# Hybrid decoder step with 32 experts: the residual summed in PSUM with the experts' rows, final norm read from PSUM, 64-column one-hot rows

## The reference

```python
t = rmsnorm(x2, ln_ffn)                      # 320 x 1024
grp = argmax(t @ rg_w + rg_b)                # one of 4 groups of 8 experts
top_v, top_i = top_k(le[grp], 2)             # two experts of that group
for e in range(32):                          # D_EXPERT = 512
    hid = silu(t @ w_gate[e]) * (t @ w_up[e])
    acc = acc + combine[:, e:e+1] * (hid @ w_down[e])
y = rmsnorm(x2 + acc, ln_final)
```

## Time and profile before

| | |
|---|---|
| median of three runs | 837.72 us |
| profiled execution | 836.28 us, span 834.6 us |
| PE busy | 780.1 us, 93% |
| DVE, ACT, POOL busy | 33%, 19%, 17% |
| granted TensorE clock, mean | 0.972 |
| read from HBM | 246.6 MB, 306 GB/s over the span |

### The profile page before, as it was taken

One profiled execution on the slowest core, in us unless ns is written; L12 is line 12 of the kernel. 1 busy time (PEld: TensorE's weight loads), 2 busy tenths in 40 slices (PEclk: granted clock), 3 DMA queues, 4 the chain that ended last, 5 costly groups with the idle time before them and its releaser, 6 DMA issues.

```text
span 834.6 us, 8869 instructions
## 1 busy us (share of the span) xinstructions
PE 780.1 (93%) x3528; PEld 376.1 (45%) x3528; DVE 274.1 (33%) x618; ACT 160.4 (19%) x321; POOL 139.5 (17%) x168
## 2 busy tenths in 40 slices
PE   4999999989899999579999999999999899999994
PEld 3777677668643335433333333333333333333331
DVE  2069999983544632511010101010101011010003
ACT  3211121333532001302111111111111121111114
POOL 2079898601002000000000000000000000000000
PEclk9999999999999999579999999999999999999998
DMA  9893200032326579588999999999999999999961
GB/s 274 306 371 121 101 20 0 9 102 107 96 88 198 172 249 411 251 309 327 425 428 427 425 428 425 427 427 425 427 428 424 429 426 427 426 426 428 428 269 64
DMA packets 50729, 249.33 MB, mean 299 GB/s; under 512 B 6886, under 2 KB 24326, under 8 KB 38127
## 3 DMA queue, kind: packets, MB, share of 16 engines
q1 hardware_dynamic: 44868, 242.75, 72.6%
q10 hardware_dynamic: 3291, 3.20, 1.3%
q0 software_dynamic: 2528, 2.79, 1.1%
HBM read 246.60 MB, written 8.61 MB: 306 GB/s over the span
## 4 chain that ended last, share of the span: by engine, by line
PE 72%; DVE 5%; issue 2%; ACT 1%; DMA 0%; ACTq 0%; POOLq 0%; DVEq 0%
PE bank L1107 27%; PE bank L1121 13%; PE bank L997 9%; PE bank L1133 8%; PE bank L1090 2%; PE bank L1115 2%; PE bank L970 1%; PE bank L961 1%; DVE bank L1472 1%; PE bank L734 1%; PE bank L986 1%; PE bank L831 1%; PE bank L1108 1%; DVE bank L1501 1%; PE bank L1040 1%
## 5 line engine op out<-in xcount | busy, mean ns | idle before, releaser
L1108 PE MATMUL bank<-ring,vy 128*64 128x512 f32 x352 | 158.1, 603 | 0.0
L734 PE MATMUL bank<-region_a,ring 128*128 128x320 f32 x576 | 157.2, 433 | 0.5 <-DVE region_a L1471 0.5
L1471 DVE TENSOR_TENSOR zz<-zz,bank 64x512 f32<-64x512 f32 x32 | 22.1, 690 | 397.6 <-ACT zz L1428 397.6
L734 PEld LDWEIGHTS bank<-region_a,ring 128*128 128x128 f32 x576 | 108.7, 190 | 46.1 <-issue 1.2
L1121 PE MATMUL bank<-ring,xcx 128*64 128x512 f32 x512 | 116.1, 595 | 1.2 <-ACT xcx L1433 1.2
L1472 DVE SCALAR_TENSOR_TENSOR bank<-region_a,par,bank 128x256 f32<-128x256 f32 x232 | 91.2, 481 | 0.0
L1107 PE MATMUL bank<-region_b,vy 128*64 128x512 f32 x176 | 79.5, 605 | 4.1 <-issue 4.1
L690 POOL DMA_INDIRECT vy<-hn_scratch,region_a x16 | 15.9, 995 | 399.9 <-PE bank L1090 353.3
L1107 PE MATMUL bank<-region_a,vy 128*64 128x512 f32 x160 | 74.1, 618 | 3.9 <-issue 3.9
L1108 PE MATMUL bank<-xcx,vy 128*64 128x512 f32 x160 | 74.2, 618 | 0.0
L997 PE MATMUL bank<-ring,vy 128*128 128x512 f32 (+1 forms) x192 | 74.0, 605 | 0.0
(11 more groups left out here) (305 smaller groups left out, 717.1 us busy)
## 6 DMA issues: line engine op xcount, KB each, us to landing
ring<-in_expert_w_down SPq DMA_DIRECT2D x31, 2048.0 KB, 29.4
ring<-in_expert_w_up SPq DMA_DIRECT2D x22, 2048.0 KB, 28.9
region_b<-in_expert_w_gate SPq DMA_DIRECT2D x11, 2048.0 KB, 25.8
ring<-in_expert_w_gate SPq DMA_DIRECT2D x10, 2048.0 KB, 24.7
region_a<-in_expert_w_gate SPq DMA_DIRECT2D x10, 2048.0 KB, 25.2
ring<-in_w_in SPq DMA_DIRECT2D x9, 2048.0 KB, 20.2
xcx<-in_expert_w_up SPq DMA_DIRECT2D x9, 2048.0 KB, 32.0
ring<-in_w_out SPq DMA_DIRECT2D x4, 2048.0 KB, 9.2
```

The costliest lines, as they stand in the source:

```text
L734: ins = pe.matmul(pt[0:m, 0:T], w[:, k, :], ht[:, k, :], start=k == 0, stop=k == KD - 1)
L1108: ins = pe.matmul(b_gu[CAP:P, :], x[:, k, :], wu[:, FE * k:FE * k + FE], **st)
L1471: tt_ = lambda out, a, b, op: dve.tensor_tensor(out, a, b, op)
```

## The change

Five things. The out product's banks are chosen as 3 to 7 and held to the end of the job list. PE writes `x2` into them by products with the identity (`residual(r)`): tile 0 ahead of the wait for `chosen`, tile 1 behind `slot_values`, the sampled tile in expert 0; every `to_tokens` then adds (start=False), in the order sampled tile, 0, 1. The final norm works bank by bank from PSUM: ACT squares 512 columns and joins partial sums by Identity and Sqrt with a bias, DVE scales each bank into `xt`, SP stores each in a DMA of its own (six). `osel` has 64 columns, `slotno` one `iota`, and `slot_values` twice six products into the two partition halves. The loads of the final gain move to SP, behind the last weight load; 256 KB are added for the sampled tile, whose column halves lie in the two partition halves.

```diff
-    until.update({name: J[("h2", 2, 0)] for name in OUT_JOBS})
+    until.update({name: len(JOBS) for name in OUT_JOBS})
...
-            b = (b + 1) % 8
-            own[wide], held[b] = b, until[wide]
+            k = 3 + OUT_JOBS.index(wide) if wide in OUT_JOBS else (b + 1) % 8
+            while held.get(k, 0) > n:
+                k = (k + 1) % 8
+            own[wide], held[k] = k, until[wide]
+            b = k
...
+            gain = A["ln_final"].rearrange("(a d) -> a d", a=1)
+            sp_.dma_start(gfin, gain.to_broadcast([P, D])).then_inc(S("gfin_in"), 16)
+            sp_.wait_ge(S("kept"), 1)
+            for q in range(2):
+                sp_.dma_start(gfin_few[TS * q:TS * q + TS, :], gain[:, 512 * q:512 * q + 512].to_broadcast([TS, 512]))\
+                    .then_inc(S("gfin_in"), 16)
...
+            def residual(r):
+                n = TILES[r][1]
+                pe.wait_ge(S("x2"), r + 1)
+                for q in range(2):
+                    dst = acc[2 * r + q][:, :] if r < 2 else acc[4][TS * q:TS * q + TS, :]
+                    ins = pe.matmul(dst, ident[0:n, 0:n], xt[0:n, r, 512 * q:512 * q + 512], start=True, stop=False)
+                return ins
+
+            residual(0)
             pe.wait_ge(S("chosen"), 1)
...
-                    ins = pe.matmul(pt[:, 0:2 * NE], osel[0:n, w, r, :],
-                                    val[0:n, w, r, :, :].rearrange("p c e -> p (c e)"), start=n_ == 0, stop=n_ == 5)
+                    for h in range(2):
+                        ins = pe.matmul(pt[CAP * h:CAP * h + CAP, 0:2 * NE], osel[0:n, w, r, :],
+                                        val[0:n, w, r, :, :].rearrange("p c e -> p (c e)"),
+                                        start=n_ == 0, stop=n_ == 5)
...
             slot_values(take(pe, "slots")).then_inc(filled, 1)
+            residual(1)
...
+                if e == 0:
+                    residual(2).then_inc(S("kept"), 1)
...
-                if e == 2:
-                    act.dma_start(gfin, A["ln_final"].rearrange("(a d) -> a d", a=1).to_broadcast([P, D]))\
-                        .then_inc(S("gfin_in"), 16)
...
+            square3(4, 0, ssq[:, 2:3])
+            part(rst[0:TS, 6:7], ssq[TS:P, 2:3], slice(TS, P))
+            part(rst[TS:P, 6:7], ssq[0:TS, 2:3], slice(0, TS))
+            root(rst[:, 2:3], ssq[:, 2:3], rst[:, 6:7], 2)
+            square3(0, 1, ssq[:, 0:1])
+            part(rst[:, 7:8], ssq[:, 0:1], slice(0, P))
+            square3(1, 2, ssq[:, 3:4])
+            root(rst[:, 0:1], ssq[:, 3:4], rst[:, 7:8], 3)
...
+            inverse3(0, 2)
+            scaled(xt[:, 2, 0:512], 4, 2, gfin_few)
+            for r in range(2):
+                inverse3(r + 1, r)
                 for q in range(2):
+                    scaled(xt[:, r, 512 * q:512 * q + 512], 2 * r + q, r, gfin[:, 512 * q:512 * q + 512])
```

More of the change, by code:

```diff
@@ L531, in _ @@
                             sp_.dma_start(ring[:, m, :], expert_src(m, e)).then_inc(S("sl_w"), 16)
[L533 to L537, removed]
+            few = O["y_sample"].rearrange("b t d -> (b t) d")
+            sp_.wait_ge(S("y_final"), 1)
+            for q in range(2):
+                sp_.dma_start(few[:, 512 * q:512 * q + 512], xt[TS * q:TS * q + TS, 2, 0:512]).then_inc(S("y_out"), 16)
+            for r in range(2):
+                for q in range(2):
+                    sp_.wait_ge(S("y_final"), 2 + 2 * r + q)
+                    sp_.dma_start(O["y_prompt"][0, TILES[r][0]:TILES[r][0] + P, 512 * q:512 * q + 512],
+                                  xt[:, r, 512 * q:512 * q + 512]).then_inc(S("y_out"), 16)
+            sp_.wait_ge(S("y_out"), 16 * 6)
             sp_.wait_ge(S("hp_out"), 16)
@@ L667, in _ @@
             pool.wait_ge(S("y_done"), 1)
[L668 to L671, removed]
+            pool.iota(slotno.rearrange("p (h j i) -> p h j i", h=2, i=2),
+                      [[CAP // 2, 2], [1, CAP // 4], [CAP // 4, 2]], base=0,
+                      channel_multiplier=0, allow_small_or_imprecise_dtypes=True)
             pool.iota(desc4, [[-1, NG]], base=NG, channel_multiplier=0, allow_small_or_imprecise_dtypes=True)
@@ L1123, in down, with to_tokens @@
                 return ins
-            def to_tokens(rows, of, first=False, end=False):
+            def to_tokens(rows, of, end=False):
                 k = rows.shape[0]
-                for r, (t0, n) in enumerate(TILES):
+                for r in (2, 0, 1):
+                    t0, n = TILES[r]
                     for q in range(2):
                         dst = acc[2 * r + q][:, :] if r < 2 else acc[4][TS * q:TS * q + TS, :]
-                        ins = pe.matmul(dst, rows[:, t0:t0 + n], of[q][0:k, :], start=first, stop=end)
-                    if end:
-                        ins.then_inc(S("summed"), 1)
+                        ins = pe.matmul(dst, rows[:, t0:t0 + n], of[q][0:k, :], start=False, stop=end)
+                        if end and (r < 2 or q == 1):
+                            ins.then_inc(S("summed"), 1)
                 return ins
@@ L1142, in combine @@
                 pe.wait_ge(S("yo"), 2 * i + 2)
-                to_tokens(back[i % 2], yo_of, first=i == 0).then_inc(S("added"), 1)
+                to_tokens(back[i % 2], yo_of).then_inc(S("added"), 1)
             pe.wait_ge(S("gath"), 16)
@@ L1449, in _, with square3, part, root @@
             act.activation(ssq[:, 6:7], ssq[:, 7:8], ACT.Sqrt)
[L1450 to L1456, removed]
+            junk = yf[:, D:D + 512]
+            def square3(m, i, to):
+                act.wait_ge(S("summed"), i + 1)
+                act.activation(junk, acc[m][:, :], ACT.Square, accum_out=to).then_inc(S("sq3"), 1)
+                act.wait_ge(S("sq3"), i + 1)
+            def part(to, of, rows):
+                act.activation(to, of, ACT.Identity, scale=1.0 / D, bias=ssq[rows, 7:8]).then_inc(S("part3"), 1)
+            def root(to, of, rest, n):
+                act.wait_ge(S("part3"), n)
+                act.activation(to, of, ACT.Sqrt, scale=1.0 / D, bias=rest).then_inc(S("rt3"), 1)
+            square3(4, 0, ssq[:, 2:3])
[6 more added lines that the diff above has]
+            root(rst[:, 0:1], ssq[:, 3:4], rst[:, 7:8], 3)
+            square3(2, 3, ssq[:, 1:2])
+            part(ssq[:, 5:6], ssq[:, 1:2], slice(0, P))
+            square3(3, 4, ssq[:, 4:5])
+            root(rst[:, 1:2], ssq[:, 4:5], ssq[:, 5:6], 4)
             act.wait_ge(S("keep_out"), 16)
@@ L1858, in _, with inverse3, scaled @@
                         ins.then_inc(S("sl_y"), 1)
-            def add_experts(r):
-                n = TILES[r][1]
-                dve.wait_ge(S("summed"), r + 1)
-                for q in range(2):
[L1865 to L1880, removed]
+            def inverse3(i, r):
+                dve.wait_ge(S("rt3"), i + 1)
+                link(dve.reciprocal(rst[:, 3 + r:4 + r], rst[:, r:r + 1]))
+            def scaled(dst, m, r, gain):
+                stt(dst, acc[m][:, :], rst[:, 3 + r:4 + r], gain, ALU.mult, ALU.mult).then_inc(S("y_final"), 1)
+            dve.wait_ge(S("gfin_in"), 48)
+            inverse3(0, 2)
+            scaled(xt[:, 2, 0:512], 4, 2, gfin_few)
+            for r in range(2):
+                inverse3(r + 1, r)
+                for q in range(2):
+                    scaled(xt[:, r, 512 * q:512 * q + 512], 2 * r + q, r, gfin[:, 512 * q:512 * q + 512])
 _INS = ["x_prompt", "x_sample", "state_conf_conv", "state_ssm_conv", "state_ssm", "ln_mix", "w_in", "conf_dw_w",
```

11 lines of the change are left out of this document (6 added, 5 removed).

## The result

| | before | changed |
|---|---|---|
| median, first comparison | 837.63 us | 828.81 us (828.51 to 830.46, four runs) |
| ratio, 95% interval | | 0.9897 [0.9879, 0.9914] |
| median, later repeat | 836.42 us | 830.03 us (828.36 to 831.56, four runs) |
| ratio, 95% interval | | 0.9926 [0.9900, 0.9951] |
| first profiled execution | 836.28 us, span 834.6 | 828.69 us, span 826.9 |

The kernel became 8.8 us faster in the first comparison and 6.4 in the repeat; the forecast was 5.7 (832.0).

A forecast was written before the change was run, and what follows sets the result against it. The weight stream was taken to bound the end of the expert stage; savings before 378.85 and behind the last weight count in full. Eight terms summed to -5.75, so 832.0 us against 837.72; range 829.2 to 835.4.

The forecast's parts named there:

- Bank order, +0.8: Output product: it now waits for DVE's read of `yoT` in bank 3, 0.8 us slower; bounds 0.8 to 2.5.
- the clock falls at the output product: Output product: a second PE stall of 0.8 brings the clock down, 1.7 us more, 833.7; 8 in 100.
- One-hot rows, -0.45: Router: `slot_select` halved to 384 elements a partition, from 0.97 to about 0.5 us; between -0.4 and -0.5.
- Rank products, -1.4: Router: `residual(0)` before `chosen` has the clock up, 12 products in 1.5 us, not 2.97; bounds 0 and -1.5.
- Slot products, -0.6: Router: 24 narrow products at half clock in 2.4 us, not 12 in 3.03; bounds +2.9 and -2.0.
- `residual(1)`, 0: Behind `slot_values`, during indices and gather: free, its clock effects put at 0; bounds -1.2 and +0.8.
- `residual(2)`, -0.9: Expert 0: the sampled tile's product half fills PE's stall before `hidden_T`; -1.7 if the clock's fall goes, 0 if not.
- Slot order, +0.4: Gather: the fullest DMA engine goes from 61 to 67 rows, 0.9 us if engine follows partition modulo 16, else 0.
- Gain loads, -1.2: Expert stage: 512 KB leave the saturated weight stream, 1.2 us; on SP behind the last weight, free; bounds 0 and -1.3.
- The tail, -2.4: Final norm: ACT sets the end, bank by bank; DVE's last scaling ends 2.4 us sooner; worked cases -2.6 and -1.4.
- The rival of table loads: Tail: if Identity and Sqrt sit in different tables, six switches cost 8.5 us in all, 840.5; 2 in 100.
- The last store, no change: End of the kernel: the last store has the same 256 KB as before, so no term was given.

The follow-up runs named there:

- the run with the gain loads: The changed kernel with all loads of the final gain (768 KB) issued on ACT's queue at expert 2: 833.86 us, 0.9940.
- the one with a fall of the clock near 797: The changed kernel with each tile of 128 rows stored whole, one DMA of 512 KB in place of two of 256 KB: 831.48 us, 0.9940.
- this pair of runs: The changed kernel with one-hot rows of 128 columns, the second half of the slots mirrored or the same way: 833.79 and 833.5 us.

## Why the prediction was wrong, step by step

- **What bounds the kernel**: right. Savings ahead of expert 3's loads shifted the stream in full: in twelve of the fourteen traces of the changed kernel and its variants (all but the run with the gain loads and the one with a fall of the clock near 797), SP's issue lies anywhere from 372.18 to 380.97, and the stretch from it to the last combine takes 440.37 to 440.82. Behind it the loads counted, as the run with the gain loads showed, though there by more than their bytes.
- **Bank order, +0.8**: measured 0.85 as a wait, 1.0 between the marks. The fall of the rival "the clock falls at the output product" is there in 5 of 11 traces with the wait. I gave it 8 in 100.
- **One-hot rows, -0.45**: -0.40 (0.97 to 0.57 in the chains of waits).
- **Rank products, -1.4**: -0.91. The clock was up for them, and PE's time fell by 1.3 us (2.96 to 1.66), nearly as priced. The failed step is the overlap: DVE's own small instructions run until 349.26, 2.08 us after the first rank product, and from there on a faster PE saves nothing. I had counted all of PE's time as DVE's wait. That the clock came up needed more than my reason: without the wait ahead of the output product it did not in two of two traces, until a further idle product stood behind tile 0's. The four instructions of `residual(0)` took 0.95 each at half clock, not 0.8, and 12 in 4.61 are 0.38 each, not 0.43; neither changed the result.
- **Slot products, -0.6**: -1.27. This is a failed step. I took half clock, rightly, and 0.1 us an instruction; 24 instructions took 1.74, 0.07 each. In the trace the two of a pair start 0.01 us apart and the next pair 0.11 later, which is the step at which L1040's unpaired ones of 64 columns go singly at the same clock (16 in 1.91). So a pair cost what I had put down for one; I had scaled from L1040.
- **`residual(1)`, 0**: -1.4, shown by taking it out, in two traces. This is the largest miss, and the other failed step: the term was put at nothing. The clock was up for the gathered rows and the first gate product in all ten traces with narrow rows and this product, where I had balanced a rise against a fall.
- **`residual(2)`, -0.9**: the fall near 371 is gone, worth 1.1 in the traces (19.4 to 18.3), but not through this product: it stays away without it. The size was right by luck, the cause was wrong.
- **Slot order, +0.4**: 0 (0.27 faster, within the 440.37 to 440.82 of the other traces). The Trainium skill ("DMA: Bandwidth & Descriptors", The descriptor swizzle), by whose blocks of four partitions the fullest engine keeps its rows, agrees with this pair of runs.
- **Gain loads, -1.2**: -1.27 in this stretch.
- **The tail, -2.4**: -2.17. Squares took 0.69 as worked out (0.60 less 0.10, and 0.19), each scaling 0.71. The rival of table loads is void: there is one load only. The Trainium skill ("ScalarE: Activation LUTs", Table sets: the hidden batching unit) has Identity in every set, and the trace agrees.
- **The last store, no change**: -0.89. I had counted bytes, which are the same 256 KB, and they alone do not set it: that store landed 2.9 us after its issue before and 2.1 in the changed kernel. What does is open.
- **Sum**: too little was put down for the slot products (0.7), `residual(1)` (1.4), the stores (0.9), the fall near 371 (0.2) and the slot order (0.4), and the first gather came 0.3 sooner by chance; on the other side stand too much for the rank products (0.5) and the tail (0.2), too little for the cost of the wait (0.2), and 0.9 of drift ahead of the change. 5.75 + 3.9 - 1.8 is 7.85, and the spans differ by 7.7. The remaining 1.1 to the first medians is the profiled execution of before, 1.35 below its median: I had noted that, and set the forecast against the median, but not widened the range for it. In the repeat the changed kernel's median was inside the range.

## What to carry to other kernels

Work for which PE has idle time anyway can be worth more than its own microseconds: an accumulator seeded by an identity product, put where indices and a gather are under way, took the clock of what follows with it; but test it by taking it out, since the same product did nothing with other neighbours. A wait for a bank costs its length and, where another gap stands close ahead of it, perhaps at times a fall of the clock that costs twice as much again (0.85 us, and 1.75 in 5 of 11 traces here). A faster engine saves only until the next thing that its reader does anyway: look at what the reader runs beside it. When a bank order is changed, give the bank whose reader is latest to the job that is needed last.

## What the runs showed of the hardware that was not expected

- Pairs of 64-column products into the two partition halves take 0.07 us an instruction at a granted clock of 0.50 (24 in 1.74); unpaired ones took 0.12 (16 in 1.91). Whether the pairs get faster at full clock no run showed.
- 768 KB of broadcast loads cost the saturated stream 3.1 us where 512 KB in rows of 4 KB cost 1.3. By subtraction, and from one trace of each, the 256 KB in rows of 2 KB cost about 1.8.
- A store of 256 KB in 128 rows of 2 KB landed 2.1 us after its issue, of 512 KB in 128 rows of 4 KB 2.7; before, 256 KB in 64 rows of 4 KB, behind two stores of 512 KB, took 2.9.
- The output product starts at 245.95 to 249.05 us in the six traces without the wait and at 247.18 to 250.38 in the eleven with it, and the work ahead of it is the same.
